# Hybrid attention trunk: norm parameters and the first weight quarter in one transfer; six warming products of 224 columns

## The reference

```python
def hybrid_layer(x, norm_g, w_in, ...):
    h = rmsnorm(x, norm_g)                 # norm_g: one gain for each channel
    (qa, ka, va, ga, qb, kb, vb, ab, gb, cq, ckv, kr, gc, mg) = split_cols(h @ w_in)
    ...
    y = m[:, :, 0] * za + m[:, :, 1] * zb + m[:, :, 2] * zc
    return x + y @ w_out

def reference(x, ...):
    for l in range(DEPTH):                 # DEPTH = 2
        x = hybrid_layer(x, norm_g[l], w_in[l], ...)
    return rmsnorm(x, final_g)
```

## Time and profile before

| | us |
|---|---|
| median of 3 runs | 922.04 (921.98 to 923.25) |
| the profiled execution, in all | 921.61 |
| its span, first to last instruction | 919.8 |
| TensorE busy in the span | 912.6 (99%) |
| VectorE busy | 613.2 (67%) |
| ScalarE busy | 390.7 (42%) |

### The profile page before, as it was taken

The page is one execution under the profiler, slowest core; times in us unless marked ns, Lnnn a source line. Parts: engine busy times, 40 slices in busy tenths (PEclk is TensorE's granted clock), DMA queues, the critical chain, the costliest instruction groups (busy, mean ns, idle before and its releaser), DMA issues.

```text
span 919.8 us, 13078 instructions
## 1 busy us (share of the span) xinstructions
PE 912.6 (99%) x5074; PEld 750.7 (82%) x5074; DVE 613.2 (67%) x1017; ACT 390.7 (42%) x726; POOL 32.3 (4%) x69
## 2 busy tenths in 40 slices
PE   9999999999999999999999999999999999999997
PEld 7988888888888777888889888888888887778886
DVE  6986468338656877575458855664567668876835
ACT  6563344225543455432444523442363435463324
POOL 0000000000000001000000000000000000100000
PEclk9999999999999999999999999999999999999999
DMA  8334325332534345422233433253235233444542
GB/s 316 101 106 130 115 70 160 95 110 80 152 115 133 93 132 161 138 91 92 92 115 95 124 93 115 69 161 103 80 115 162 102 115 116 130 148 137 151 124 91
DMA packets 46989, 111.02 MB, mean 121 GB/s; under 512 B 12656, under 2 KB 15760, under 8 KB 46800
## 3 DMA queue, kind: packets, MB, share of 16 engines
q1 hardware_dynamic: 40928, 100.72, 34.6%
q10 hardware_dynamic: 3920, 5.25, 2.1%
q0 software_dynamic: 2080, 4.22, 1.6%
HBM read 85.43 MB, written 2.24 MB: 95 GB/s over the span
## 4 chain that ended last, share of the span: by engine, by line
PE 99%; DMA 0%; ACT 0%; issue 0%; DVE 0%; POOLq 0%
PE ring L689 76%; PE nat L689 9%; PE nat L898 3%; PE aux L921 2%; PE nat L877 1%; PE nat L704 1%; PE nat L703 1%; PE nat L706 1%; PE ring L704 1%; PE ring L703 1%; PE ring L706 1%; PE nat L782 1%; DMA par_all<-params 0%; PE ring L759 0%; PE ring L769 0%; PE nat L849 0%
## 5 line engine op out<-in xcount | busy, mean ns | idle before, releaser
L689 PE MATMUL ring<-act_hi,w_hi 128*128 128x512 f32 x784 | 307.5, 392 | 0.0
L689 PE MATMUL ring<-act_lo,w_hi 128*128 128x512 f32 x784 | 305.4, 390 | 0.0
L689 PE MATMUL ring<-act_hi,w_lo 128*128 128x512 f32 x784 | 305.2, 389 | 0.0
L938 ACT ACTIVATE w_hi<-raw 128x1024 fp32r<-128x1024 f32 x152 | 161.5, 1064 | 330.2 <-PE ring L689 257.4
L1279 DVE TENSOR_TENSOR w_lo<-raw,w_hi 128x1024 fp32r<-128x1024 f32 x152 | 184.6, 1216 | 98.2 <-ACT w_hi L938 98.0
L689 PEld LDWEIGHTS ring<-act_hi,w_hi 128*128 128x128 f32 x784 | 147.1, 188 | 37.3 <-issue 7.3
L689 PEld LDWEIGHTS ring<-act_hi,w_lo 128*128 128x128 f32 x784 | 147.1, 188 | 31.1
L689 PEld LDWEIGHTS ring<-act_lo,w_hi 128*128 128x128 f32 x784 | 147.2, 188 | 29.7
L1665 DVE SCALAR_TENSOR_TENSOR gates<-ring,rstd 128x512 f32<-128x512 f32 x72 | 49.4, 686 | 79.2 <-PE ring L689 79.0
L689 PE MATMUL ring<-y_hi,w_hi 128*128 128x512 f32 x192 | 74.9, 390 | 0.0
L689 PE MATMUL ring<-y_hi,w_lo 128*128 128x512 f32 x192 | 74.7, 389 | 0.0
(11 more groups left out here) (240 smaller groups left out, 1040.4 us busy)
## 6 DMA issues: line engine op xcount, KB each, us to landing
raw<-pieces SPq DMA_DIRECT2D x152, 512.0 KB, 3.5
bank_g<-work SPq DMA_DIRECT2D x80, 64.0 KB, 2.6
lat<-work SPq DMA_DIRECT2D x48, 64.0 KB, 2.7
bank_g<-work POOLq DMA_DIRECT2D x40, 64.0 KB, 2.4
bank_g<-work ACTq DMA_DIRECT2D x40, 64.0 KB, 3.2
xt<-x_t SPq DMA_DIRECT2D x8, 256.0 KB, 5.3
bank_a<-work SPq DMA_DIRECT2D x32, 64.0 KB, 2.0
bank_g<-bank_a SPq DMA_DIRECT2D x16, 128.0 KB, 3.9
```

Of the source, the lines that this page charges most:

```text
L689: mm = pe.matmul(dst, stationary, moving, start=start and i == 0, stop=stop and i == 2)
L938: nc.scalar.activation(w_hi[:, n % HL, :], raw[:, n % RAW, :], ACT.Copy).then_inc(hi_split.sem, 1)
```

## The change

The parameters and the first quarter of the first weight piece become one array `first` of 128 rows by 40 + 256 numbers, made on the host. In the core's memory `par_all` and `raw` become views of one tile, `loaded`, in which they lie side by side, so that ScalarE's first transfer fetches both into neighbouring places. GpSimd's transfer, the semaphore `par_loaded` and ScalarE's wait for it (L980) go; the wait for the first weight quarter, which stands ahead of it on ScalarE, covers both. The other three quarters come as before. TensorE's warming products go from five with 256 columns to six with 224.

```diff
@@ -50,7 +50,7 @@
-WARM = 5
+WARM = 6
@@ -317,7 +317,9 @@
-        raw = sb("raw", [P, RAW, 1024])
+        loaded = sb("loaded", [P, DEPTH * PARAMS + RAW * 1024])
+        par_all = loaded[:, 0:DEPTH * PARAMS].rearrange("p (l n) -> p l n", l=DEPTH)
+        raw = loaded[:, DEPTH * PARAMS:].rearrange("p (r n) -> p r n", r=RAW)
@@ -333,7 +335,6 @@
-        par_all = sb("par_all", [P, DEPTH, PARAMS])
@@ -420,7 +421,7 @@
-        par_loaded, setup_loaded = sig("par_loaded", 0), sig("setup_loaded", 0)
+        setup_loaded = sig("setup_loaded", 0)
@@ -788,7 +789,7 @@
             for _ in range(WARM):
-                pe.matmul(aux[:, 0:256], warm[:, 0:P], warm[:, 0:256], start=True, stop=True)
+                pe.matmul(aux[:, 0:224], warm[:, 0:P], warm[:, 0:224], start=True, stop=True)
@@ -957,7 +958,10 @@
                 p, cols = HEADS[n]
-                act.dma_start(raw[:, p, cols], pieces[p, :, cols]).then_inc(head_loaded[n].sem, 16)
+                if n == 0:
+                    act.dma_start(loaded[:, 0:DEPTH * PARAMS + cols.stop], first).then_inc(head_loaded[n].sem, 16)
+                else:
+                    act.dma_start(raw[:, p, cols], pieces[p, :, cols]).then_inc(head_loaded[n].sem, 16)
@@ -977,7 +981,6 @@
             head_hi_part(0)
-            act.wait_ge(par_loaded.sem, 16)
@@ -1227,7 +1230,6 @@
-            pool.dma_start(par_all[:, :, :], params).then_inc(par_loaded.sem, 16)
@@ -1881,10 +1883,11 @@
+    pieces = pack_pieces(w_in, w_oa, w_ob, w_oc, w_uq, w_ukv, w_out)
...
-        "pieces": pack_pieces(w_in, w_oa, w_ob, w_oc, w_uq, w_ukv, w_out),
-        "params": params,
+        "pieces": pieces,
+        "first": np.concatenate([params.reshape(P, DEPTH * PARAMS), pieces[0, :, 0:256]], axis=1),
```

More of the change, by code:

```diff
@@ L305, in at, with build_hybrid_trunk @@
         return layer * self.per_layer + (self.before + max(n, 1 - self.before))
-def build_hybrid_trunk(nc, x_t, pieces, params, alpha, tables, consts, final_g, out, k_rope_dram, ends_dram):
+def build_hybrid_trunk(nc, x_t, pieces, first, alpha, tables, consts, final_g, out, k_rope_dram, ends_dram):
     with ExitStack() as ctx:
```

## The result

The changed kernel took 939.06 us (median of 5, 938.82 to 939.15), the kernel before 921.98 in the same comparison (921.70 to 923.25): a ratio of 1.0184, 95% interval 1.017 to 1.0198. The forecast was 921.4 with a range up to 922.6. So it is slower by 17 us, and nothing in the prediction leads there. The profiled execution took 938.84, with a span of 937.0.

A forecast was written before the change was run, and what follows sets the result against it. TensorE bounds the kernel, busy 912.6 of 919.8 us; only its 0.7 us start wait was reachable. The x split 0.74 earlier, capped by the chain at 0.60, gave 922.04 - 0.60 = 921.4; range 920.8 to 922.6.

The forecast's parts named there:

- Merged transfer: Kernel start: 20 KB more in ScalarE's first transfer costs 0.08 us; first x split starts at 4.88, 0.74 earlier.
- nothing else moves there: GpSimd's queue: nothing waits behind its dropped first transfer before the attention blocks, so dropping it moves nothing else there.
- The rival of a late transfer: Kernel start: merged transfer takes up to 0.58 more, x split at 5.38, gain 0.24, time 921.8; chance 0.10.
- the rule cited there from the Trainium skill: Kernel start: the issuing engine gains a transfer only sequencer time, so the merge saves 0.53, not 0.74; time 921.5.
- The warming products: Kernel start: twelve records at 0.389 us, the last at 5.47; first product at 5.86, 0.11 later, third product unaffected.
- TensorE's lead and the cap: TensorE leads by 0.74 or a little more; by 38 us the VectorE/ScalarE chain caps the gain at 0.56 to 0.65.
- ScalarE's split of 17.34: Head of the chain to 37.7: its 0.56 us wait for TensorE goes, so it starts 0.56 to 0.65 earlier.
- The weight load of 37.75: End of the chain: comes at 37.1 to 37.2, with a wait for VectorE longer than 0.19 us.
- I take 0.60: At 38 us: gain taken from the chain's 0.56 to 0.65, reaching the end, 922.04 - 0.60 = 921.4.
- so its work up to 16.8 stays where it is: ScalarE's split of piece 2 at 13.46 waits 0.52 us for a transfer, so ScalarE gains nothing up to 16.8.
- The clock rival: First products run at the low clock: 921.5 for a rise at 6.5; 6.5 to 9 us 0.17, later 0.04 (to 924.2).

The follow-up runs named there:

- the two kernels with the layout mended: Changed kernel with merged tile allocated behind con: 921.23 us; changed kernel with 96 bytes left free in front of the parameters: 921.33 us.
- the padded one: Changed kernel with 96 bytes left free in front of the parameters, weights 256 bytes further than before; 921.33 us against 922.07 for before, 0.9989.
- the other kernel: Changed kernel, merged transfer and six warming products kept, with the merged tile allocated behind con; 921.23 us against 921.96 for before, 0.999.
- The kernel of one moved allocation: Kernel before with only the parameters' tile moved, between raw and w_hi, so weights lie 160 bytes further; 940.57 us, ratio 1.0198.
- the three kernels with the merged transfer and the layout in step: Changed kernel with merged tile behind con, 921.23 us; the same with five warming products of 256 columns, 921.21; changed kernel with 96 bytes free, 921.33.
- the kernel moved by 512 bytes: Kernel before with a 512-byte tile (ones_r) allocated between raw and w_hi; 921.73 us, ratio 0.9993.
- that with 128 bytes: Kernel before with a 128-byte tile (sink_exp) allocated between raw and w_hi; 939.29 us, ratio 1.0186.

## Why the prediction was wrong, point by point

**The step that failed** is the part "Merged transfer". It counts what moves: the transfer, GpSimd's issue, ScalarE's wait, the first splits. That "nothing else moves there" is true of GpSimd's queue; of the partition the prediction says nothing, so the merge of the tiles was costed at nothing. But the diff takes 40 columns from the end of the partition and puts them in front of `raw`, and every tile from there to the parameters' old place, weights and `y` among them, moves by 160 bytes against the activations. That cost 6.3 ns for each of 2772 products, 17.5 us. No term of the sum and no rival held that move, so no range made from the rivals could hold the time. The forecast of what was costed can be read from the two kernels with the layout mended, 921.23 and 921.33 against a forecast of 921.4.

**The merged transfer itself** was priced right. After starts its first weight split at 4.53 (forecast 4.57), its first split of x at 4.86 (4.88). The rival of a late transfer didn't come; nor did the 0.53 that the rule cited there from the Trainium skill would have left: the split of x came 0.76 earlier than in the earlier trace rows.

**The warming products** were off by a little. Twelve records came, 0.373 apart behind the first and not 0.389 (the 0.444 that it scales is a mean with a first interval of 0.59 in it; the others are 0.427), and the last two at the higher level. In the timeline of after, those two:

```profile
5.08 0.54 PE L792 MATMUL aux<-merged 128*128 128x224 f32 x2
```

Two that are 0.373 apart do not fit into 0.54 us, since one alone, of 256 columns, took 0.63 at the lower level; these are 0.19 apart. The first product starts at 5.71, not 5.86. L770 starts at 6.40 (forecast 6.44), as it should if the longer warming doesn't reach it.

**TensorE's lead and the cap** have to be read where the layout is mended. ScalarE's split of 17.34 starts at 16.55 in one and 16.65 in the other of these two kernels, 0.79 and 0.69 earlier where 0.56 to 0.65 were forecast; in the padded one it still waits, against the forecast, for TensorE:

```profile
16.65 1.06 ACT L939 ACTIVATE w_hi<-loaded 128x1024 fp32r<-128x1024 f32 x1 [0.34 <-PE ring L770]
```

The weight load of 37.75 comes 0.79 and 0.69 earlier as well; in the same kernel:

```profile
37.06 0.19 PEld L690 LDWEIGHTS nat<-w_hi,act_hi 128*128 128x128 f32 x1 [0.20 <-DVE w_lo L1281]
```

The chain moved as far as TensorE and not less, so the wait didn't grow, and the term "I take 0.60" came out at 0.79 and 0.69. The step behind it that failed is "so its work up to 16.8 stays where it is": the transfer that ScalarE's split of piece 2 waits for, at 13.46 in the earlier trace rows, does not land at a fixed time. In the padded kernel that split starts 0.47 earlier:

```profile
12.99 1.06 ACT L939 ACTIVATE w_hi<-loaded 128x1024 fp32r<-128x1024 f32 x1 [0.55 <-DMA loaded<-pieces]
```

So ScalarE was ready before TensorE there, and the split followed TensorE's lead (L770 starts 0.68 earlier). In the other kernel it starts at 13.31, 0.15 earlier, and 0.15 with the forecast's 0.65 makes the 0.79. In after it starts later:

```profile
13.83 1.06 ACT L939 ACTIVATE w_hi<-loaded 128x1024 fp32r<-128x1024 f32 x1 [0.56 <-DMA loaded<-pieces]
```

There the split comes at 17.06, without a wait for TensorE, and the load at 37.45, 0.28 and 0.30 earlier than before: 0.65 less the 0.37 by which the transfer was late. Of the lead of 0.78 that L770 had, TensorE kept 0.52 at its run of 24 (17.40 against 17.92), since its products were slower already.

**The clock rival** named a real mechanism, but in the timings the late rise comes with the kernel before and not with the merged transfer. With five warming products and the merged transfer the first three products did run at the lower level, up to 6.9, and the run of 24 started 0.52 earlier than before (17.40), near the 0.45 to 0.55 that it priced for a rise at 6.5. The rest is told below.

## What to carry to other kernels

Before a tile grows, shrinks or moves, list which tiles are allocated behind it, and pad so that the tiles that large products read stay whole multiples of 256 bytes apart, the weight tiles among themselves too (shown here for 128 by 128 weights and 512 columns in fp32r); a small tile belongs behind the large ones, or gets filled up to 256 bytes. A merge of two transfers is a change of layout too, and the layout is costed like any other part of the diff. When busy time of an engine grows with no new instruction, compare groups of the same shape that read different tiles: the one that stays as it was tells what the others have in common.

## What the hardware showed that was not expected

**The time of a product depends on how far apart the tiles lie that TensorE reads.** The size: 4 to 7 ns on 227 for a 512-column product in fp32r whose tiles aren't 256 bytes apart in whole numbers, up to 2.2% of this kernel's time. The 432-column products, 0.197 apart in both kernels, didn't show it. The Trainium skill, page "SBUF — State Buffer", section "Who interferes with whom", says that "PE and ACT never wait on anyone"; and the page "TensorE: Matmul & The Clock Gate", section "Step-by-step: what each phase is for", that loading the next weights takes no read bandwidth from the running product. No other engine is needed for the loss here: the 114 intervals of activation products in after during which neither another engine nor a transfer was at work average 233.3 ns, and the 108 such intervals of before 226.8. The kernel of one moved allocation issues the same instructions. By these two pages the kernels that differ only in where their tiles lie would have taken the same time. The measurements decide against that.

**The clock's rise comes at the start, at no fixed moment.** In after the products pass from the lower level (1.2 GHz) to the higher (2.4 GHz) at about 5.1 us, under the warming; in the kernel with five warming products and the merged transfer at about 6.9; in the kernel with the new warming alone at about 10.6, seen in the distance of its products:

```profile
8.91 0.63 PE L769 MATMUL ring<-act_lo,w_hi 128*128 128x512 f32 x1
9.34 0.63 PE L759 MATMUL ring<-act_hi,w_hi 128*128 128x512 f32 x1
...
10.88 0.40 PE L766 MATMUL ring<-act_hi,w_lo 128*128 128x512 f32 x1
11.11 0.39 PE L769 MATMUL ring<-act_lo,w_hi 128*128 128x512 f32 x1
```

They start 0.43 apart up to 10.6 and 0.23 behind it; ahead of them TensorE had been without work for 0.6 us, waiting for the split of x. The tenth product starts at 10.62, against 8.91 in the profiled execution of before: 1.71 later, and this execution took 923.33 in all, against 921.61: 1.72 more. The timings of the kernel before fall into two groups: of 79 taken beside the experiments 47 lie between 921.5 and 922.4 and 32 between 923.0 and 924.0, with none in between, and the means of the two lie 1.55 apart. Of 32 timings of the three kernels with the merged transfer and the layout in step none is above 921.7. So the merged transfer seems to do more than its 0.7 us: with it the late rise goes. A gap without work can cost the level: in the kernel moved by 512 bytes the warming is at the higher level from 4.2, then TensorE waits 2.1 us, and after two products it is at the lower level again, until about 11. The timeline, and a window of that stretch in the form of the earlier trace rows:

```profile
7.16 0.47 PE L759 MATMUL ring<-act_hi,w_hi 128*128 128x512 f32 x1 [2.12 <-ACT act_hi L970]
...
7.90:10.50 2.60, 2.60 (x7) 2.10 (x7) 2.60 (x6) 2.60 (x7) 0.00 (x0) 0.50 1.05 402
```

The granted clock reads 0.50 there. It reads 1.00 in the slow products of the kernel with the new warming alone, so the distance of the products is the surer sign. That the merged transfer works by shortening the gap is argued from the counts and a few profiles; no run changed the gap alone, and its length does not decide by itself: the gap is 0.7 in the profile of before and 0.5 in that with 128 bytes, where the rise came only after 10. A median hides all this: of the 79 it is 922.0, the mean 922.4, and the mean of the 32 is 921.25.
